# A hybrid decoder block: expert weights from the fifth expert on in 4 MB units with 32 KB runs, a one-expert first gather, and the end in small pieces

## The reference

```python
logits = (t @ router_w + router_b).astype(jnp.float32)
top_v, top_i = lax.top_k(logits, TOP_K)          # 4 of 32
top_w = jax.nn.softmax(top_v, axis=-1)
combine = jnp.einsum('tk,tke->te', top_w, jax.nn.one_hot(top_i, N_EXPERTS))
for e in range(N_EXPERTS):
    a = clamped_swiglu(t @ w_gate_up[e] + b_gate_up[e])     # 1024 x 2048, then 1024 wide
    out = out + combine[:, e:e + 1] * (a @ w_down[e] + b_down[e])   # 1024 x 1024
...
return rms_norm(x, final_norm_w)
```

## Time and profile before

| | |
|---|---|
| three runs, us | 1293.10, 1288.21, 1290.36; median 1290.36 |
| profiled execution | 1289.13 us, span 1287.4 us |
| PE busy | 1213.8 us, 94% of the span |
| DVE, ACT, POOL busy | 34%, 22%, 8% |
| moved by the DMA | 454.03 MB, 353 GB/s over the span |
| granted TensorE clock | 0.994 in the mean |

### The profile page before, as it was taken

One profiled execution on the slowest core, in us unless ns is written; L12 is line 12 of the kernel. 1 busy time (PEld: TensorE's weight loads), 2 busy tenths in 40 slices (PEclk: granted clock), 3 DMA queues, 4 the chain that ended last, 5 costly groups with the idle time before them and its releaser, 6 DMA issues.

```text
span 1287.4 us, 16612 instructions
## 1 busy us (share of the span) xinstructions
PE 1213.8 (94%) x6657; PEld 626.7 (49%) x6657; DVE 441.5 (34%) x914; ACT 280.4 (22%) x503; POOL 105.3 (8%) x89
## 2 busy tenths in 40 slices
PE   6999999999899999999998989898999989898985
PEld 6999987778744344343442423232332324232422
DVE  7966566776532222122221212212221212222113
ACT  4673438663310011010110101010110101000101
POOL 1301301354600000000000000000000000000000
PEclk9999999999989999999999999999999999999999
DMA  7647434327989999999999999999999999999994
GB/s 228 212 131 230 132 102 145 115 99 238 397 335 399 430 425 430 428 428 430 426 430 428 428 430 426 430 429 428 431 426 430 429 428 430 427 429 428 426 430 207
DMA packets 70745, 454.03 MB, mean 353 GB/s; under 512 B 10160, under 2 KB 34864, under 8 KB 46128
## 3 DMA queue, kind: packets, MB, share of 16 engines
q1 hardware_dynamic: 67744, 451.30, 85.6%
q10 hardware_dynamic: 2960, 2.17, 0.7%
HBM read 452.40 MB, written 1.05 MB: 352 GB/s over the span
## 4 chain that ended last, share of the span: by engine, by line
PE 59%; DMA 32%; DVE 4%; ACT 3%; issue 1%; POOL 0%; ACTq 0%; DVEq 0%; SPq 0%
DMA ring<-in_w_gate_up_dram 29%; PE psum L1086 20%; PE psum L1100 10%; PE psum L793 9%; PE psum L1075 5%; PE psum L758 4%; PE psum L1126 3%; DMA ring<-in_w_down_dram 3%; PE psum L796 2%; PE psum L720 2%; DVE WL L1532 1%; ACT WH L1227 1%; PE psum L1003 1%; PE psum L1057 1%; PE psum L874 1%
## 5 line engine op out<-in xcount | busy, mean ns | idle before, releaser
L1086 PE MATMUL psum<-ring,ZS 128*64 128x512 f32 x1504 | 355.3, 616 | 13.3 <-DMA ring<-in_w_gate_up_dram 13.3
L1086 PEld LDWEIGHTS psum<-ring,ZS 128*64 128x64 f32 x1504 | 100.2, 135 | 229.1 <-issue 192.4
L1976 DVE TENSOR_TENSOR X<-X,psum 128x1024 f32<-128x1024 f32 x64 | 75.3, 1217 | 387.5 <-PE psum L1126 387.5
L1100 PE MATMUL psum<-ring,HT 128*64 128x512 f32 x784 | 176.4, 596 | 20.3 <-DMA ring<-in_w_down_dram 19.6
L1960 DVE TENSOR_SCALAR ZS<-psum 128x512 f32<-128x512 f32 x32 | 22.1, 692 | 316.0 <-PE psum L1086 316.0
L1086 PE MATMUL psum<-slot,ZS 128*64 128x512 f32 x528 | 123.8, 615 | 2.0 <-DMA slot<-in_w_gate_up_dram 2.0
L1100 PEld LDWEIGHTS psum<-ring,HT 128*64 128x64 f32 x784 | 54.5, 137 | 129.6 <-issue 104.6
L1532 DVE TENSOR_TENSOR WL<-ring,WH 128x2048 fp32r<-128x2048 f32 (+1 forms) x42 | 97.1, 2315 | 43.3 <-ACT WH L1227 43.2
L1451 ACT ACTIVATE HT<-psum 128x512 f32<-128x512 f32 x32 | 19.1, 597 | 324.5 <-PE psum L720 324.5
L1227 ACT ACTIVATE WH<-ring 128x2048 fp32r<-128x2048 f32 (+1 forms) x42 | 78.6, 1875 | 11.2 <-PE psum L758 7.2
L1086 PEld LDWEIGHTS psum<-slot,ZS 128*64 128x64 f32 x528 | 35.8, 135 | 73.3 <-issue 64.6
(11 more groups left out here) (336 smaller groups left out, 1184.6 us busy)
## 6 DMA issues: line engine op xcount, KB each, us to landing
ring<-in_w_gate_up_dram SPq DMA_DIRECT2D x94, 2048.0 KB, 33.7
ring<-in_w_down_dram SPq DMA_DIRECT2D x49, 2048.0 KB, 35.1
slot<-in_w_gate_up_dram SPq DMA_DIRECT2D x33, 2048.0 KB, 33.8
ring<-in_w_in_dram SPq DMA_DIRECT2D x30, 1024.0 KB, 5.6
slot<-in_w_down_dram SPq DMA_DIRECT2D x15, 2048.0 KB, 35.0
ring<-in_w_branch_ssm_dram SPq DMA_DIRECT2D x4, 1024.0 KB, 5.1
ring<-in_w_branch_nsa_dram SPq DMA_DIRECT2D x4, 1024.0 KB, 4.9
ring<-in_w_out_dram SPq DMA_DIRECT2D x4, 1024.0 KB, 5.1
```

Of the source, the lines that this page charges most:

```text
L1086: ins = mm(psum[64 * (c % 2):64 * (c % 2) + 64, c // 2, :], XTS[:, k, s], every_other_pair(w[:, 2048 * (k % 2):2048 * (k % 2) + 2048], c), ...
L1100: ins = mm(psum[64 * h:64 * h + 64, 2, :], lhs, w[:, at:at + 512], start=(j + hf + k == 0), stop=(j == 1 and hf + k == 2))
L1976: v.tensor_tensor(xo, xo, psum[:, 3 + 2 * t:5 + 2 * t, :], ALU.add).then_inc(o_read, 1)
```

## The change

The slots are now four of 4 MB. From the fifth expert on a unit is a transfer of 4 MB: 512 rows of gate-up weights or all of an expert's down weights, 128 partitions of 32 KB each, in one run. PE reads a unit in two halves and waits once for it; SP waits for both halves of the unit that the slot held before. For experts 0 to 3 the same slots are filled half by half, with 2 MB pieces that are half of each 32 KB run; PE's code for these experts is written out ahead of the loop (`four(0)`). Because a partition now holds four (or eight) neighbouring rows instead of two (or four), the gathers and transposes read every fourth column instead of every second.

The first gather is split: DVE writes the two parts of SPR for expert 0 first, PE gathers expert 0 alone (64 columns), does two pieces, and gathers expert 1 then. The last down unit comes in pieces of 1, 1, 1, 0.5 and 0.5 MB with a semaphore each; expert 31's transposes move between the halves of expert 30's down product, and the combines of experts 30 and 31 stand behind all products and add up in PSUM, so that DVE adds once. The last norm takes the two row blocks one after the other.

```diff
-BIG = 2 * SLOT
-SLOTS = 8
+BIG = 4 * SLOT
+HALF = BIG // 2
+SLOTS = 4
 GU_U, DN_U = 4, 2
 PAIR = 2 * (GU_U + DN_U)
 PERIOD = 2 * PAIR
-ONCE = SLOTS
-FIRST_SLOT = (0, 1, 2, ONCE)
-LOOP_SLOT = tuple((n + 3) % SLOTS for n in range(PERIOD))
+UNITS_4 = PERIOD // 2
+LOOP_SLOT = tuple((n + 2) % SLOTS for n in range(UNITS_4))
+FIRST_HALVES = {(0, 0): 1, (0, 1): 1, (1, 0): 1}
+LAST_ROWS = ((0, 2), (2, 4), (4, 6), (6, 7), (7, 8))
...
+            def gate_up_rows(e, ab):
+
+                return w_gate_up[0, e, 512 * ab:512 * ab + 512, :].rearrange("(p k) n -> p (k n)", k=4)
+
+            def down_rows(e):
+
+                return w_down[0, e].rearrange("(p k) n -> p (k n)", k=8)
+
+            def unit_rows(unit, e, nxt):
+
+                h, n = unit // 6, unit % 6
+                if n < 2:
+                    return gate_up_rows(e + (2 * h + 1), n)
+                if n == 2:
+                    return down_rows(e + 2 * h)
+                if n < 5:
+                    return gate_up_rows(nxt if h else e + 2, n - 3)
+                return down_rows(e + (2 * h + 1))
...
+            def load_half(rows, slot, hi):
+
+                part_of = slice(HALF * hi, HALF * hi + HALF)
+                sp.dma_start(places[slot][:, part_of], rows[:, part_of]).then_inc(half_full[slot][hi], 16)
...
+            sp.dma_start(once, gate_up_rows(0, 1)[:, HALF:BIG]).then_inc(once_full, 16)
+            for n, (unit, hi) in enumerate(((2, 0), (2, 1), (3, 0))):
+                sp.wait_ge(unit_done, NU + n + 1)
+                early_load(unit, hi)
+            for n in range(8, PERIOD):
+                sp.wait_ge(unit_done, units_to(0, n - 7))
+                early_load(n // 2, n % 2)
...
-                for pos in range(PERIOD):
-                    sp.wait_ge(unit_done, units_to(i * 2, pos - SLOTS + 1))
-                    load_at(pos, (i % EX4) * 4, ((i + 1) % EX4) * 4, LOOP_SLOT[pos])
-            for n, pos in enumerate((*range(PAIR + 6), PERIOD - 2, PERIOD - 1)):
-                sp.wait_ge(unit_done, units_to(last * 2, n - SLOTS + 1))
-                load_at(pos, EXPERTS - 4, 0, LOOP_SLOT[n])
+                for unit in range(UNITS_4):
+                    sp.wait_ge(unit_done, units_to(i * 2, 2 * unit - 6))
+                    slot = LOOP_SLOT[unit]
+                    sp.dma_start(places[slot], unit_rows(unit, (i % EX4) * 4, ((i + 1) % EX4) * 4)
+                                 ).then_inc(half_full[slot][0], 16)
+            for unit in range(9):
+                sp.wait_ge(unit_done, units_to(last * 2, 2 * unit - 6))
+                slot = LOOP_SLOT[unit]
+                sp.dma_start(places[slot], unit_rows(unit, EXPERTS - 4, 0)).then_inc(half_full[slot][0], 16)
+            for (r0, r1), full in zip(LAST_ROWS, last_full):
+                if r0 % 4 == 0:
+                    sp.wait_ge(unit_done, units_to(last * 2, 11 + r0 // 4))
+                sp.dma_start(places[LOOP_SLOT[9]][:, D * r0:D * r1], down_rows(EXPERTS - 1)[:, D * r0:D * r1]
+                             ).then_inc(full, 16)
...
-                        first = 256 * (k // 2) + k % 2
-                        ins = mm(bank(5 + k // 4, P, off=P * (k % 4)), H2[:, t, first:first + 255:2],
+                        first = 512 * (k // 4) + k % 4
+                        ins = mm(bank(5 + k // 4, P, off=P * (k % 4)), H2[:, t, first:first + 509:4],
...
+            def landed(i, unit, hi):
+
+                slot = LOOP_SLOT[unit]
+                if isinstance(i, int) and i == 0:
+                    pe.wait_ge(half_full[slot][hi], early_loads(unit, hi))
+                elif hi == 0:
+                    pe.wait_ge(half_full[slot][0], loop_loads(i, unit))
+                return places[slot]
...
+            def gather_one(s, full):
+
+                for k in range(KT):
+                    for t in range(T):
+                        first = 512 * (k // 4) + k % 4
+                        ins = mm(bank(5 + k // 4, CAP, off=256 * s + CAP * (k % 4)), H2[:, t, first:first + 509:4], SPR[:, t, s],
+                                 start=(t == 0), stop=(t == T - 1))
+                    if k % 4 == 3:
+                        ins.then_inc(full, 1)
 
             pe.wait_ge(h2_ready, 4)
-            gather(1)
+            pe.wait_ge(spr_first, 1)
+            gather_one(0, first_full)
             for j in range(GU_U):
-                pe.wait_ge(xte_ready, 1 if j < 2 else 2)
-                gate_up(0, j, FIRST_SLOT[j], 16)
+                pe.wait_ge(first_in, 1 if j < 2 else 2)
+                if j < 3:
+                    pe.wait_ge(half_full[j // 2][j % 2], 16)
+                    gate_up(0, j, places[j // 2])
+                else:
+                    pe.wait_ge(once_full, 16)
+                    gate_up(0, j, once, HALF)
                 if j == 1:
+                    pe.wait_ge(spr_ready, 1)
+                    pe.wait_ge(first_in, 2)
+                    gather_one(1, xte_full)
                     pe.wait_ge(cw_ready, 1)
                     for t in range(T):
                         ins = tr(bank(4, T, P)[:, t], CWP[:, t].rearrange("p a b -> p (a b)"))
                     ins.then_inc(cwt_full, 1)
+            pe.wait_ge(xte_ready, 2)
...
+            four(0)
+            with pe.Fori(1, last) as i:
+                four(i)
             odd_half(last * 2, last, 0, False)
             even_half(last * 2, last, 0)
-            odd_half(last * 2 + 1, last, PAIR, True)
-            combine(last * 4 + 3, 0)
-            act_turned(last * 4 + 4)
+            odd_half(last * 2 + 1, last, 6, True)
             pe.wait_ge(at_ready, last * 4 + 4)
-            for j in range(DN_U):
-                down(j, LOOP_SLOT[PAIR + 6 + j], loop_loads(last, PAIR + 6 + j))
-            combine(last * 4 + 4, 1)
+            for (r0, r1), full in zip(LAST_ROWS, last_full):
+                pe.wait_ge(full, 16)
+                w = places[LOOP_SLOT[9]]
+                for r in range(r0, r1):
+                    for h in range(2):
+                        ins = mm(psum[64 * h:64 * h + 64, 0, :], ATL[:, r // 2, 64 * (r % 2):64 * (r % 2) + 64],
+                                 w[:, D * r + 512 * h:D * r + 512 * h + 512], start=(r == 0), stop=(r == 7))
+                if r1 % 4 == 0:
+                    ins.then_inc(unit_done, 1)
+            combine(last * 4 + 3, 0, final=False)
+            combine(last * 4 + 4, 1, YSL2, first=False)
...
-            gathers((0, 0), (0, 1), (1, 0), (1, 1))
+            gathers((0, 0), (1, 0))
+            own.settle()
+            dve.sem_inc(spr_first, 1)
+            gathers((0, 1), (1, 1))
...
+                act.wait_ge(ss_ready, 3 + t)
+                a(ss[:, 2 + t:3 + t], ss[:, t:t + 1], ACT.Sqrt, scale=1.0 / D, bias=ss[:, 6:7]).then_inc(sq_root, 1)
...
+                dve.wait_ge(sq_root, 3 + t)
+                v.reciprocal(ss[:, 4 + t:5 + t], ss[:, 2 + t:3 + t]).then_inc(lg_ready, 1)
+                dve.wait_ge(lg_ready, 2 + t)
```

More of the change, by code:

```diff
@@ L324, in hybrid_block @@
         XTS = part(ZS, 0, KT, 2, CAP)
+        ATL = part(ZS, 0, 4, P)
+        YSL2 = part(ZS, 512, 512)
         SGA = part(ZS, 1024, 512)
@@ L451, in units_to, with loop_loads, early_loads @@
             return pair * PAIR + (NU + GU_U + n)
-        def loop_loads(i, pos):
-            slot = LOOP_SLOT[pos]
-            before = LOOP_SLOT[:pos].count(slot) + FIRST_SLOT.count(slot)
-            return i * (16 * LOOP_SLOT.count(slot)) + 16 * (before + 1)
+        def loop_loads(i, unit):
+            slot = LOOP_SLOT[unit]
+            n = LOOP_SLOT.count(slot)
+            before = FIRST_HALVES.get((slot, 0), 0) + n + LOOP_SLOT[:unit].count(slot)
+            return (i - 1) * (16 * n) + 16 * (before + 1)
+        def early_loads(unit, hi):
+            slot = LOOP_SLOT[unit]
+            return 16 * (FIRST_HALVES.get((slot, hi), 0) + LOOP_SLOT[:unit].count(slot) + 1)
         def rounds(eng):
@@ L1078, in gather, with gate_up, down @@
                         ins.then_inc(xte_full, 1)
[L1080 to L1083 removed]
+            def landed(i, unit, hi):
+                slot = LOOP_SLOT[unit]
+                if isinstance(i, int) and i == 0:
[3 more added lines that the diff above has]
+                return places[slot]
+            def gate_up(s, j, w, first=0):
                 for k in (2 * j, 2 * j + 1):
                     for c in range(4):
+                        at = 2048 * (k % 4) - first
                         ins = mm(psum[64 * (c % 2):64 * (c % 2) + 64, c // 2, :], XTS[:, k, s],
[L1087 to L1088 removed]
+                                 every_other_pair(w[:, at:at + 2048], c), start=False, stop=(k == KT - 1))
                 ins.then_inc(unit_done, 1)
[L1091 to L1101 removed]
+            def down(j, w):
+                for k in range(4 * j, 4 * j + 4):
+                    lhs = ATS[:, k // 2, 64 * (k % 2):64 * (k % 2) + 64]
+                    for h in range(2):
+                        at = 1024 * k + 512 * h
```

(32 more changed lines are left out.)

128 lines of the change are left out of this document (40 added, 88 removed).

## The result

The changed kernel took **1305.01 us** (median of 4 runs, 1304.55 to 1307.73), the kernel before 1291.13 beside it (4 runs, 1288.21 to 1293.1). The ratio is 1.0113, 95% interval 1.0099 to 1.0128: 1.1% slower. Forecast were 1287.4 and a range of 1280.5 to 1293.6.

A forecast was written before the change was run, and what follows sets the result against it. PE bounds the kernel until the issue at 404.62 us, then the full weight stream. Rate -6.0, start +2.8, coarser units 0 and end +0.2 sum to -3.0, giving 1287.4 us against a median of 1290.36; range 1280.5 to 1293.6.

The forecast's parts named there:

- the start: PE work up to the 404.62 us issue, mainly the split first gather: +2.8 us, between +1.0 and +4.0.
- the bound of 0.7 us: Upper end for reading the stationary tokens at a step of 4 instead of 2 before 404.62 us; +0.1 taken.
- a microsecond added after it costs nothing: PE work after the issue at 404.62 us is free, since the weight queue grows 4.6 us per expert pair.
- Rival (c): Long runs are slower: at 421 GB/s the 81 units take 807 instead of 794 us, 1306 total; chance 0.08.
- The signs that I had named: Start: third unit's issue (373.55 us before) about 2.7 us later, the first (365.83) 0.7 us earlier.
- until the granted clock goes from 0.50 to 1.00 at 361: First gather: 0.20 us per instruction until full clock at 361 us, 0.1 after; ends at 361.3 instead of 362.0.
- The hole in the stream: First loop issues: no window between 460 and 490 us with a DMA share below 0.97.
- Coarser units: Loop issues wait for both halves, PE for 4 MB instead of 2: 0 us, at worst +1 to +2.
- The rate, -6.0: 81 weight units with 32 KB runs save 9.2 ns per packet avoided: 431 instead of 428 GB/s, -6.0 us.
- Rival (a): Longer runs save little because 428 GB/s is the memory's rate or overheads overlap: 1290 to 1294 us; chance 0.17.
- rival (b): Loss is per transfer as well as per packet and goes altogether, up to -11 us: 1279.5 to 1284.5; chance 0.21.
- The end, +0.2: After expert 30's down weights land: first DVE addition +1.25, norm by row blocks about -1.05; +0.2 us (-0.5 to +1).

The follow-up runs named there:

- e3: Kernel before, with only the gathers' token reads changed from a step of 2 to 4 (wrong columns, same counts): 1297.44 us, ratio 1.0051.
- e1: Changed kernel, with GpSimd storing the tokens in reading order so the gathers read at a step of 1: 1289.46 us, ratio 0.9993 to the kernel before.
- e4: Changed kernel with tokens stored for a step of 1 and one full first gather of both experts: 1284.04 us, ratio 0.9953 to the kernel before.
- e2: Changed kernel with one full first gather of 128 columns instead of the split, step of 4 kept: 1292.54 us, ratio 1.0017 to the kernel before.
- e5: e4 with each 4 MB unit loaded as two 2 MB transfers of 16 KB runs: 1290.99 us, ratio 1.0001 to the kernel before.
- e6: e4 with each unit still one 4 MB transfer, but two 16 KB runs per partition: 1290.92 us, ratio 1.0004 to the kernel before.
- e7: e4 with the last down unit in two 2 MB pieces instead of five: 1284.09 us, ratio 0.9952 to the kernel before.

## Why the prediction was wrong

**The step that failed** stands in the part on the start: "Transposes of HT (stride 2) have weight loads of 208 ns against 141 for QT (stride 1); for the one full gather and the transposes before 404.62 I take +0.1 (0 to 0.7)". I had priced the gather's operand by a row of another operation, and by the distance of steps 1 and 2 at that; and that row does not measure the step, for at a step of 4 the same transposes have loads of 212 ns. The earlier trace rows had the operand itself, 196 ns at a step of 2; no row showed a step of 4, so the bound of 0.7 us had nothing under it. The runs put in its place **a load of 330 ns for 196, and 3.7 us more for each full gather**, in all of the loop and not only ahead of 404.62. In the kernel before that alone costs 6.7 us (e3, 1297.44 against 1290.79 on the same chip); in the changed kernel, taking it back gives 15.6 us and a time within my range (e1).

The Trainium skill has a rule that would have warned, and I had not weighed it: "Advanced Engine Details and Errata", section "SBUF Cachelines", says that SBUF has lines of 16 bytes and that at least two hits on one are needed for full speed. By that rule steps of 4 and 8 bytes are free, 12 is dearer, and 16 and 32 cost the same, with one hit each; the gathers agree at every point (192, 196, 261, 329 and 335 ns). The transposes of HT do not: a step of 16 bytes leaves them at 212 ns. The Trainium skill's page "TensorE: Matmul & The Clock Gate", section "LDWEIGHTS (loading the stationary operand)", which I did cite, lets the load depend on its columns alone; 192 to 335 ns for the same 128 columns do not agree.

**What hung on it.** The sentence "a microsecond added after it costs nothing" held only up to 4.8 us per pair, and I never asked whether the change used this up. The gathers took 3.7 of them, and the faster stream 0.5 (58.8 to 58.3 us). What was left, 0.6, is below what the filled slots cover over 15 pairs, so the gain of the faster stream could not be cashed: the rest stays at 911.7 us, where e1 and e4, with the same stream, have 905.5 and 905.7. Rival (c) gave about the measured time, 1306, for a wrong reason: the rate rose.

**The start,** +2.8 forecast and 14.6 in the traces. Without the 0.9 of a later first gather, 13.7 remain, where my sum had 3.3 without the 0.5 of an earlier one. They are, piece by piece in the chain of the changed kernel against the kernel before: first gather 7.70 for 6.42, +1.3 instead of -0.2; first two pieces 9.91 for 7.35, +2.6 instead of 0; second gather +7.7 instead of +3.4; next two pieces 9.51 for 7.38, +2.1 instead of 0. So 5.7 of the 10.4 us that I missed lie in the two gathers, each 7.7 us by the step alone, and 4.7 in four pieces that partly ran at half clock. The signs that I had named show it too: the third unit was issued 14.6 us later (388.15 for 373.55), not 2.7, and the first not earlier but 4.8 us later (370.60 for 365.83).

Beside the step, the term that I had mis-sized here is "until the granted clock goes from 0.50 to 1.00 at 361". In the changed kernel the clock was back at 1.00 only from 370 on, 5.4 us after the first gather had ended, in e1 from 364 on, 2.4 us after. In all ten kernels with one first gather of 128 columns it was back before this gather ended. And in the changed kernel it fell once more in the second gather and stayed at 0.50 from 380 to 386, which it did not in e1, nor in the gathers of the loop, which cost the same 7.66 us with 128 columns. The pairs e4 and e1, e2 and the changed kernel differ by the split alone, so it is the split that goes with the longer half clock; what in it does so, no run isolates. With cheap loads the split costs 5.4 us by the medians (6.2 in the "between" column), against +3.4 for the second gather and 0.2 less for the first in my sum.

**The hole in the stream.** I had said that no window from 460 to 490 would be below 0.97; 480 to 490 shows 0.87 in the changed kernel, 480 to 500 0.90, and 420 to 440 0.82. That is not the 4 MB units, which e4 has too (1.02 and 1.01), but PE's lateness. "Coarser units: 0" stands: e5 and e6, which keep the coarse waits and the new end and give up only the runs, are at 1.0001 and 1.0004 of the kernel before. One thing I had not foreseen: PE's waits for weights get fewer and longer. From 620 to 1262 the kernel before waits 53 times, 1.2 us at most, and the clock stays at 1.00; e4 waits 22 times, up to 2.1 us, and the clock falls to 0.50 for some 3 us now and then (1064 to 1066, 1122 to 1124, 1180 to 1182). The totals of e5 and e6 show no cost of this; that the longer waits bring the falls was not tested.

**The rate, -6.0.** Right: 431 forecast, 432 measured, and 6.9 us by e4, and by e7 on the same chip, against e5 and e6. The 9.2 ns per packet out of one 1 KB stretch and one 16 KB stretch proved good to some 15% (10.6). Rival (a) is refuted by these pairs. Of rival (b), the part per transfer is refuted: e6 has it and gains nothing. The 3 cycles per packet of the Trainium skill's "DMA: Bandwidth & Descriptors", "Why small descriptors are slow (HBM only)", give an estimate of 3.5 ns, a third of the 10.6 saved.

**The end, +0.2.** The small pieces are worth nothing, as forecast (e7). That expert 30's down weights decide holds in e7 only: the changed kernel waits for no weights at all, and in e1 and e4 the last wait is for a gate-up unit before them. From their landing to the first addition of DVE e7 shows 1273.56 - 1255.81 = 17.75 us, before 16.87: +0.9 instead of +1.25. From that addition to the end of the span the changed kernel takes 8.9 us (1303.4 - 1294.54) instead of 9.95 (1287.4 - 1277.45): -1.1, as forecast. So -0.2 in sum.

With the stride repaired, my other terms would have been nearly enough: e1 is at 1289.46 for a forecast of 1287.4, and 2.0 us of the difference lie in the start, where the first gather takes 7.06 us for some 6.2 and the next two pieces 8.51 for 7.35, at half clock.

## What to carry to other kernels

Who lengthens the runs of a weight transfer changes which rows of the contraction share a partition, and with it the step at which the other operand is read: look at the stationary side of the matmul first, and let the engine that writes that tile store it in reading order (here free of charge on GpSimd, e1 and e4). A second engine that is "hidden anyway" is so by a number of microseconds per iteration; write it down (4.8 here) and charge every edit of the loop body against it. And splitting a gather by its moving columns doubles its price: 32 products took 3.71 us with 64 columns in e1 and 3.77 with 128, and at a step of 4 they took 7.66 with either.

## What was not expected of the hardware

The stationary load's dependence on the step (192, 196, 261, 329, 335 ns at 4, 8, 12, 16, 32 bytes), while the transposes of HT, where the change widened the step as well, kept theirs, 212 for 208 ns; why these are spared was not tried. Long runs still pay at sizes where I had half expected nothing: 16 KB to 32 KB took the stream from 428 to 432 GB/s, and halving the number of transfers did nothing. At a step of 4 the clock did not matter to a gather (7.70 us at 0.50, 7.66 at 1.00). And the granted clock stayed at 0.50, or fell to it, in stretches in which PE shows no idle time at all: for 4 to 6 us at the start of every first gather, until 370 and again from 380 to 386 in the changed kernel, until 364 in e1, the long ones only with the split gathers. What the chip counts there stays open.
